# Hybrid HGRN2 and differential-attention block on one core: the order of the first loads, and half of two modulation parts as direct matmuls

## The reference

```python
mod = silu(c) @ w_ada + b_ada
shift, scale, gate = split(mod, 3)
h = rms_norm(x, g_pre) * (1.0 + scale) + shift
proj = h @ w_in          # 6144 columns: hq hf hi hg dq dk dv dg ma mb
# branch A: HGRN2, chunked recurrence, per-head RMSNorm, * silu(hg)
# branch B: differential causal attention, per-head RMSNorm, * silu(dg)
y = sigmoid(ma) * (o_a @ w_branch_a) + sigmoid(mb) * (o_b @ w_branch_b)
x = x + gate * rms_norm(y @ w_out, g_post)
```

## Time and profile before

| | |
|---|---|
| time, median of 3 runs | 908.14 us (908.01 to 912.44) |
| profiled execution: time | 908.02 us |
| profiled execution: span of the trace | 906.2 us |
| mean granted TensorE clock | 0.989 |
| TensorE matmul busy | 853.7 us, 94% |
| VectorE busy | 575.3 us, 63% |
| ScalarE busy | 441.5 us, 49% |
| GpSimd busy | 447.8 us, 49% |

### The profile page before, as it was taken

The page is one execution under the profiler, slowest core; times in us unless marked ns, Lnnn a source line. Parts: engine busy times, 40 slices in busy tenths (PEclk is TensorE's granted clock), DMA queues, the critical chain, the costliest instruction groups (busy, mean ns, idle before and its releaser), DMA issues. The chain is left out here.

```text
span 906.2 us, 12968 instructions
## 1 busy us (share of the span) xinstructions
PE 853.7 (94%) x4829; PEld 671.6 (74%) x4829; DVE 575.3 (63%) x691; ACT 441.5 (49%) x808; POOL 447.8 (49%) x348
## 2 busy tenths in 40 slices
PE   2899899999999999999999999999999999999996
PEld 2678677777777777777777777777788788778885
DVE  3888984788684897866886948746200622982222
ACT  7676322885445865437864446754445700321111
POOL 6054665455555445654454555556788564730000
PEclk9899899999999999999999999999999999999999
DMA  9914221102110120121021021201321731111231
GB/s 329 327 48 140 70 70 47 48 1 71 47 48 24 47 70 1 48 70 46 3 71 47 2 69 47 69 10 39 101 62 46 279 140 47 35 59 47 102 108 70
DMA packets 74481, 68.10 MB, mean 75 GB/s; under 512 B 3700, under 2 KB 65204, under 8 KB 74420
## 3 DMA queue, kind: packets, MB, share of 16 engines
q1 hardware_dynamic: 74304, 67.25, 23.0%
q10 hardware_dynamic: 116, 0.03, 0.0%
HBM read 58.88 MB, written 8.39 MB: 74 GB/s over the span
## 5 line engine op out<-in xcount | busy, mean ns | idle before, releaser
L595 POOL TENSOR_TENSOR w_lo<-w_raw,w_hi 128x512 fp32r<-128x512 f32 x140 | 193.0, 1380 | 261.4 <-ACT w_hi L1144 259.9
L879 PE MATMUL pj<-b_hi,w_hi 128*128 128x512 f32 x616 | 263.0, 427 | 2.7 <-DVE dk L1467 1.5
L881 PE MATMUL pj<-b_hi,w_lo 128*128 128x512 f32 x616 | 242.2, 393 | 0.0
L880 PE MATMUL pj<-b_lo,w_hi 128*128 128x512 f32 x616 | 241.8, 392 | 0.0
L879 PEld LDWEIGHTS pj<-b_hi,w_hi 128*128 128x128 f32 x616 | 116.4, 189 | 40.1 <-issue 10.2
L881 PEld LDWEIGHTS pj<-b_hi,w_lo 128*128 128x128 f32 x616 | 116.2, 189 | 26.2
L880 PEld LDWEIGHTS pj<-b_lo,w_hi 128*128 128x128 f32 x616 | 116.8, 190 | 22.7 <-issue 3.8
L1144 ACT ACTIVATE w_hi<-w_raw 128x512 fp32r<-128x512 f32 x132 | 82.8, 628 | 64.0 <-PE pj L881 57.6
L576 POOL TENSOR_TENSOR w_raw<-w_raw,w_raw 128x512 f32<-128x512 f32 x66 | 91.8, 1391 | 2.9
L1159 ACT ACTIVATE p<-sp,cols 128x1024 f32<-128x1024 f32 (+7 forms) x64 | 46.8, 737 | 0.8
L1301 ACT ACTIVATE y_hi<-y 128x1024 fp32r<-128x1024 f32 x8 | 8.5, 1062 | 74.8 <-DVE y L1668 74.8
(11 more groups left out here) (250 smaller groups left out, 1709.9 us busy)
## 6 DMA issues: line engine op xcount, KB each, us to landing
w_raw<-in_w_in SPq DMA_DIRECT2D x96, 256.0 KB, 4.1
x_in<-in_x SPq DMA_DIRECT2D x8, 512.0 KB, 7.1
ada<-in_w_ada SPq DMA_DIRECT2D x16, 256.0 KB, 7.0
ada<-in_w_ada SPq DMA_DIRECT2D x8, 512.0 KB, 8.0
ada_g<-in_w_ada SPq DMA_DIRECT2D x8, 512.0 KB, 3.8
wo_raw<-in_w_out SPq DMA_DIRECT2D x8, 512.0 KB, 4.0
res<-in_x SPq DMA_DIRECT2D x8, 512.0 KB, 4.2
out_x<-y2n SPq DMA_DIRECT2D x8, 512.0 KB, 2.9
```

The lines of the kernel that those rows point to most:

```text
L595: pool.tensor_tensor(w_lo[slot(v)][:, :], raw[:, :], w_hi[slot(v)][:, :].bitcast(F32), ALU.subtract).then_inc(s_wlo, 1)
L879: pe.matmul(bank[:, :], wh, part(b_hi[m], kk), start=(fresh and kk == 0), stop=False, skip_group_check=True)
L880: pe.matmul(bank[:, :], wh, part(b_lo[m], kk), start=False, stop=False, skip_group_check=True)
L881: last = pe.matmul(bank[:, :], wl, part(b_hi[m], kk), start=False, stop=(kk == 3), skip_group_check=True)
```

## The change

The loads are issued in another order: four tiles of x, weights of group 0, piece 0 of w_ada, weights of group 1, piece 1, then the second half of x, then (behind a wait for s_modp, the first columns of the modulation) piece 2 and the rest. In pieces 0 and 1 half of the row tiles (4 to 7, and 0 to 3) are no longer summed by VectorE; TensorE multiplies them itself with one column of silu(c), as sixteen matmuls of one column per piece, and sums in PSUM. Piece 1 gets another PSUM bank. Transposes of the first half run tile by tile as the tiles are scaled; two warming matmuls come earlier. The second half of x is squared, scaled, transposed and used later, with products of j = 0 and 1 between its transposes; the products of kh = 1 for j = 0 and 1 have kk outside. ScalarE takes the fourth tile's scaling and starts with a Sqrt.

```diff
+DIRECT = [[4, 5, 6, 7], [0, 1, 2, 3]]
+ADDS = [4, 8, 16]
...
-        XT_BANKS = [0, 1, 2, 3, 4, 5, 6, 0, 4, 5, 6, 4, 5, 6, 4, 5]
+        mod_banks = [mod_bank, first_banks[0][1], mod_bank]
+        XT_BANKS = [0, 1, 2, 3, 4, 5, 6, 0, 6, 4, 5, 6, 6, 6, 6, 6]
...
+            load_x(0)
+            load_half(0, 0)
+            load_piece(0)
+            load_half(1, 0)
+            load_piece(1)
+            load_x(1)
+            sp_.wait_ge(s_modp, 1)
+            load_piece(2)
...
+            def mod_direct(p, kk):
+                a, b = PIECES[p]
+                pe.wait_ge(s_ada[p][kk // 2], 32)
+                for z in range(2):
+                    for e in range(a, b):
+                        c0 = z * P * (b - a) + P * (e - a)
+                        last = pe.matmul(mod_banks[p][:, KT * z + e:KT * z + e + 1], ada[p][kk][:, c0:c0 + P], c_silu[:, kk:kk + 1],
+                                         start=(kk == DIRECT[p][0] and z == 0 and e == a), stop=False, skip_group_check=True)
...
-            for n in range(KT):
-                x_block(n)
-            pe.wait_ge(s_const, N_CONST)
-            pe.wait_ge(s_vec, 1)
-            mod_columns(0)
-            pe.wait_ge(s_xt, KT)
             for _ in range(2):
                 pe.matmul(first_banks[3][0], ident[:, :], sc[:, 0:HALF], start=True, stop=True)
+            for t in range(4):
+                if t == 3:
+                    pe.wait_ge(s_xnb, 1)
+                else:
+                    pe.wait_ge(s_xna, t + 1)
+                for n in range(KT - 1):
+                    last = pe.transpose(xt_bank[n][:, t * P:(t + 1) * P], x_in[:, t * D + n * P:t * D + (n + 1) * P], ident[:, :])
+                    if t == 3:
+                        last.then_inc(s_xtr, 1)
+                if t == 1:
+                    pe.wait_ge(s_gain, 1)
+                if t >= 1:
+                    mod_direct(0, DIRECT[0][t - 1])
+            mod_direct(0, DIRECT[0][3])
+            mod_columns(0)
+            x_block(KT - 1)
+            pe.wait_ge(s_const, N_CONST)
+            pe.wait_ge(s_xt, 5)
+            for kk in DIRECT[1]:
+                mod_direct(1, kk)
+            pe.wait_ge(s_xt, KT)
...
-                elif kk < 3:
-                    for n in range(4):
-                        x_block(KT + 4 * (kk - 1) + n)
-            mod_columns(2)
+            for n in range(4):
+                x_block(KT + n)
+            pe.wait_ge(s_xt, KT + 3)
+            for kk in range(4):
+                pe.wait_ge(s_bl, 4 + kk + 1)
+                for j in range(2):
+                    last = first_product(j, 0, 1, kk)
+                    if kk == 3:
+                        last.then_inc(s_proj, 1)
+                x_block(KT + 4 + kk)
+                if kk == 1:
+                    mod_columns(2)
             pe.wait_ge(s_xt, 2 * KT)
-            for j in range(4):
+            for j in range(2, 4):
...
-            for j, th in ((0, 0), (1, 0), (0, 1), (1, 1)):
-                pe.wait_ge(s_wlo, 5 + j)
+            for th in range(2):
                 for kk in range(4):
-                    if j == 0:
-                        pe.wait_ge(s_bl, 8 + 4 * th + kk + 1)
-                    last = first_product(j, 1, th, kk)
-                last.then_inc(s_proj if th else s_first, 1)
+                    pe.wait_ge(s_bl, 8 + 4 * th + kk + 1)
+                    for j in range(2):
+                        if kk == 0 and th == 0:
+                            pe.wait_ge(s_wlo, 5 + j)
+                        last = first_product(j, 1, th, kk)
+                        if kk == 3:
+                            last.then_inc(s_proj if th else s_first, 1)
...
+            act.activation(t_o, ones[:, 0:1], ACT.Sqrt)
+            for t in range(4):
+                square(t)
+            root(0)
...
+            scale_x(3)
+            act.activation(t_o, ones[:, 0:1], ACT.Sqrt)
+            for n in range(KT):
+                x_out(n)
+            act.wait_ge(s_mod, 1)
+            blocks(0, 1)
+            blocks(1, 2)
+            square(4)
+            square(5)
+            act.wait_ge(s_mod, 2)
+            blocks(2, 4)
+            for t in range(6, NT):
                 square(t)
             root(1)
             act.wait_ge(s_rsq, 2)
+            scale_x(7)
+            x_out(KT)
+            blocks(4, 5)
+            for n in range(KT + 1, KT + 3):
                 x_out(n)
+            blocks(5, 6)
+            x_out(KT + 3)
+            x_out(KT + 4)
+            blocks(6, 7)
+            x_out(KT + 5)
+            blocks(7, 8)
+            x_out(KT + 6)
+            x_out(KT + 7)
             act.wait_ge(s_mod, 3)
             blocks(8, 16)
...
             norm(0)
             dve.wait_ge(s_rsq, 1)
+            scale_x(0)
+            scale_x(1)
+            dve.wait_ge(s_sigc, 1)
+            then(dve.tensor_tensor(c_silu, c_col, c_sig, ALU.mult))
...
+            scale_x(2)
+            for kk in range(4):
                 add_ada(0, kk)
             mod_piece(0)
+            add_ada(1, 4)
             block_low(0)
             add_ada(1, 5)
             block_low(1)
             add_ada(1, 6)
             add_ada(1, 7)
+            mod_piece(1)
+            block_low(2)
+            block_low(3)
             add_ada(2, 0)
             add_ada(2, 1)
+            norm(1)
+            dve.wait_ge(s_rsq, 2)
+            for t in range(4, 7):
+                scale_x(t)
+            for kk in range(2, 4):
+                add_ada(2, kk)
+            block_low(4)
             add_ada(2, 4)
             add_ada(2, 5)
+            block_low(5)
             add_ada(2, 6)
             add_ada(2, 7)
+            block_low(6)
+            block_low(7)
             mod_piece(2)
```

More of the change, by code:

```diff
@@ L477, in _, with load_x, load_piece @@
             w_mod = w_ada[0, :, 0:2 * D].rearrange("k (z f) -> k z f", z=2)
-            for half in range(2):
+            def load_x(half):
                 for t in range(4 * half, 4 * half + 4):
                     sp_.dma_start(x_in[:, t * D:(t + 1) * D], x_v[t * P:(t + 1) * P, :]).then_inc(s_xl[t], 16)
-                load_half(half, 0)
-            for p, (a, b) in enumerate(PIECES):
+            def load_piece(p):
+                a, b = PIECES[p]
                 for kk in range(KT):
-                    if p == 2 and kk == 0:
-                        sp_.wait_ge(s_acc, KT)
                     sp_.dma_start(ada[p][kk][:, :].rearrange("p (z f) -> p z f", z=2),
                                   w_mod[kk * P:(kk + 1) * P, :, a * P:b * P]).then_inc(s_ada[p % 2][kk // 2], 16)
+            load_x(0)
[6 more added lines that the diff above has]
+            load_piece(2)
             for half in range(2):
@@ L799, in mod_columns @@
                         c0 = 2 * P * a + z * P * (b - a) + P * (e - a)
-                        last = pe.matmul(mod_bank[:, KT * z + e:KT * z + e + 1], acc[:, c0:c0 + P], ones[:, 0:1],
-                                         start=True, stop=True)
+                        last = pe.matmul(mod_banks[p][:, KT * z + e:KT * z + e + 1], acc[:, c0:c0 + P], ones[:, 0:1],
+                                         start=(p == 2), stop=True, skip_group_check=True)
                 last.then_inc(s_modp, 1)
@@ L999, in blocks @@
                 block_high(e1 - 1)
-            square(0)
-            square(1)
+            act.wait_ge(s_const, 3)
+            act.activation(t_o, ones[:, 0:1], ACT.Sqrt)
+            for t in range(4):
+                square(t)
+            root(0)
             act.wait_ge(s_vec, 1)
@@ L1007, in _ @@
             act.activation(one_less_lb, lb_diff, ACT.Sigmoid, scale=-1.0).then_inc(s_sigc, 1)
-            square(2)
-            square(3)
-            root(0)
-            for t in range(4, NT):
+            act.wait_ge(s_rsq, 1)
+            scale_x(3)
[10 more added lines that the diff above has]
+            for t in range(6, NT):
                 square(t)
@@ L1014, in _ @@
             act.wait_ge(s_rsq, 2)
-            for n in range(4):
+            scale_x(7)
+            x_out(KT)
+            blocks(4, 5)
+            for n in range(KT + 1, KT + 3):
                 x_out(n)
-            scale_x(4)
-            x_out(4)
-            x_out(5)
-            scale_x(5)
-            x_out(6)
-            x_out(7)
-            act.wait_ge(s_mod, 1)
-            blocks(0, 2)
-            scale_x(6)
-            scale_x(7)
-            act.wait_ge(s_mod, 2)
-            blocks(2, 4)
-            for n in range(KT, KT + 4):
-                x_out(n)
-            blocks(4, 5)
-            for n in range(KT + 4, 2 * KT):
-                x_out(n)
-            blocks(5, 8)
+            blocks(5, 6)
[6 more added lines that the diff above has]
+            x_out(KT + 7)
             act.wait_ge(s_mod, 3)
@@ L1376, in _ @@
             dve.wait_ge(s_rsq, 1)
-            for t in range(4):
-                scale_x(t)
-            norm(1)
-            for kk in range(KT):
+            scale_x(0)
```

(13 more changed lines are left out.)

43 lines of the change are left out of this document (17 added, 26 removed).

## The result

The changed kernel takes 914.40 us (median of 9 runs, 912.91 to 917.44) against 908.44 for the kernel before (9 runs, 906.75 to 912.44). The ratio is 1.0059, 95% interval 1.0041 to 1.0078 (ratios here are formed from all the runs; that of the two medians would be 1.0066). The profiled execution took 913.71 us at a span of 911.8; the one of before 908.02 at 906.2. So the forecast of 906.4 and its range up to 911.5 are missed on the slow side.

The account below looks back on a forecast made before the run. DVE's unbroken run from M6's low part (76.03) to PE's wait ending at 97.88 was taken to bound the kernel. Starting it at 74.4 gained 1.6 us: span 906.2 to 904.6, plus 1.8 outside, 906.4 us; range 902.6 to 911.5.

Parts of the forecast that it names:

- Direct columns: TensorE's one-column matmuls for the modulation: 0.12 us each assumed, range up to 0.22, from a row of 16 lasting 1.95.
- Start: Loads to first product: first columns near 18, first product at 22.2 against 31.08, 8.9 us earlier.
- Loads: Loading phase: first half of x at 8.0 us, part 0 by 15, part 1 by 22, second half of x by 28.
- Middle: From mod_columns(1) at 26.8 to ACT's blocks 8 to 15 at 53.1, 2.9 us later than before.
- The spell at the low clock: In the middle, after mod_columns(2)'s sixteen columns: one slow-clock spell adding 1.6 us before blocks 8 to 15.
- Blocks 8 to M6: From blocks 8 at 53.1 to DVE's M6 low part at 74.4: 21.3 us, the kh = 1 order delaying the q copy.
- From there to the end: From M6's low part to the end: DVE never waits until 97.88, so 1.6 us gained there reaches the end.
- forecast lead of 1.6 us: At DVE's M6 low part: start at 74.4 instead of 76.03, taken whole off the span.
- Slow middle: Rival, PE from 38 to 58 us: low clock between bursts of two products, +3.1 us, 911.1 us; chance 0.13.
- The low spell moves: Rival: clock falls near 85 ahead of L740, spell after 97.88 goes, 1.6 + 3.3 us gained, 903.1; chance 0.08.
- The lead passes whole: Rival: hidden DVE slack between 76 and 98, so PE's own 3.7 us gain counts, 902.6 us; chance 0.10.
- Nothing arrives: Rival: loads 2 us later than estimated, or a second short low-clock spell, 908.2 us; chance 0.15.

Follow-up runs that it names:

- second experiment: The changed kernel with no direct columns at all, VectorE summing parts 0 and 1 wholly: 916.05 us, ratio 1.0063.
- the one execution with a trace: The kernel before with ScalarE making M6's high part before forget(0, 1) instead of after it: 909.28 us, ratio 0.9990.
- the warmed version: The changed kernel with part 1 summed by VectorE and two 512-column warming matmuls ahead of the first product: 911.35 us, ratio 1.0017.

## Why the prediction was wrong, step by step

The step that failed is the start, up to mod_columns(1), which stood in the sum at 26.8 and came at 32.8. In it the direct columns were mis-sized: sixteen were priced at 1.9 us and took 3.4 in part 0, and those of part 1, which have no term of their own in the sum, took 6 us, of which 2.0 to 3.8 us arrived. The place that passes a loss on, M6's low part, was named rightly.

The parts of the change, each by what M6's low part does when it alone is added to the version above it:

| version | M6's low part at, us | step | time, us | ratio |
|---|---|---|---|---|
| kernel before | 76.03 | | | 1 |
| new loads alone | 81.35 | +5.3 | 914.82 | 1.0052 |
| and direct columns of part 0 | 79.31 | -2.0 | 911.59 | 1.0031 |
| and the new middle | 78.11 | -1.2 | 910.70 | 1.0017 |
| and direct columns of part 1 (the changed kernel) | 80.08 (again: 81.50) | +2.0 (+3.4) | 914.40 | 1.0059 |

The steps sum to 4.05 and are of single executions. Three executions with the same start have their first product at 26.55, 27.61 and 29.16, so a step of 1 or 2 us is no more than a sign; the ratios of the runs have the same order, and give +4.7, -1.9, -1.3 and +3.8 us for the four steps. The direct columns of part 0 are worth 4.0 with the new middle (second experiment) and 2.0 with the old one (3.0 where blocks 8 start); why a third of it is lost between there and M6 in the old order stays open. The step "new middle" includes the new order of the kh = 1 products.

**Direct columns, the term that was mis-sized.** I took sixteen for 1.9 us, since a row "x16" lasted 1.95. An f32 matmul is two records, so sixteen are 32 records: 3.4 us at the full clock (part 0: 0.88, 0.81 and 1.71 us) and 5.3 to 6.8 us where the clock falls (part 1). The count could have been had from the rows of before: four columns of `mod_columns(0)` in the code stand as x8. For the columns of part 1 the sum has no term: its 22.2 for the first product goes through ACT and DVE, as if they lay wholly in PE's wait for the first low part. That wait covers 3 of the 6 us: the low part started at 23.84 and took 0.69, the first product came at 27.61. So 3 us remained in this execution, 3.4 against the version with an equally early fall of the clock, 3.8 by the ratios.

**Start.** First columns at 20.3 to 21.2 in place of 18: the direct columns of part 0 cost 1.5 us more by the same count, PE waited 0.91 us for part 0's loads, and DVE's product for silu(c) took 1.23 us and so held the third tile. Without part 1's columns the first product starts at 25.6, so at most 3.4 of the 5.4 us by which it came late are here, and 2.0 or more are part 1's columns. The chain from the end of part 0's columns over affine, high and low part takes 4.1 us there (21.5 to 25.6), near the 4.2 that I had. The low clock over the first twelve matmuls of the products was nowhere in the sum: mod_columns(1) came 5.2 us behind the first product, and I had 4.6.

**Loads.** DVE's first sum of part 1 waited for its load until 23.00, where the same rate as in the sum (part 1 in by 22) gives 20.6; the first tile of the second half of x was there at 27.11, where it gives 23.4. So they were 2.4 and 3.7 us late. In the changed kernel this was hidden: ACT, which had waited 1.94 us for x, waited 4.63 more for part 1's columns afterwards, and these were released by PE.

**Middle.** From mod_columns(1) to blocks 8 I had 26.3 us, measured 25.2. The four waits of PE that I had as 1.9, 0.65, 0.55 and 0.8 are 1.82, 0.36, 0.43 and 0.69 (a fifth is 0.19). The spell at the low clock (1.6 us) did not come. But I had only compared the end with the old one, 53.1 with 50.25, and read the 2.9 us as a detail of PE's and ACT's order. The run with the new loads alone shows 5.2 us at this point. That they come from the work on the later half of x is read from DVE's and ACT's rows there; no run moved that half by itself (the run also has the transposes row group by row group and ACT's new start). The direct columns of part 0 pay back a part of it.

**Blocks 8 to M6.** 21.3 forecast, 22.1 measured. The order of kh = 1 was charged with 2 us and saves 1.8; that the sum was nearly right here is luck. Forecast 74.4, measured 80.08: +6.0 at mod_columns(1), -1.1 in the middle, +0.8 here.

**From there to the end.** That M6's low part passes delays on holds in the rows: +2.36 becomes +2.3 in the span, +4.05 stays 4.07 up to 442 us, and ten of thirteen traces take 362.0 to 362.6 us from there to the copy of q. For leads, on which the forecast rested, it stays open: -3.04 became -0.7 in the one execution with a trace, but by a low clock that the kernel before shows without a lead. What the forecast lead of 1.6 us would have been worth can't be said from these runs.

**Rivals.** *Slow middle* fell for the changed kernel, whose clock stays 1.00 from 38 to 58. The waits between its bursts were 0.19 to 1.82 us. The page of the Trainium skill that the forecast cited ("TensorE: Matmul & The Clock Gate", section "HAM oscillation — how this bites in real kernels") tells of waits of about 3 to 5 us, so the middle here is no test of it; I had stretched it to shorter ones. In the warmed version one wait of 1.82 was followed by 0.73 over 6 us. At the start the clock fell between 20.3 and 22.7, where PE had had no wait since 15.5 at the latest, in or behind rows of one-column matmuls. So it did in the kernel before: the forecast named half a microsecond of idle time ahead of the sixteen columns' row at 47.87, but PE idled 0.11 us in the 4.9 us ahead of it, and the clock fell at 50.0. *The low spell moves* came half true: PE no longer waits 3 us at L753, but waits 2.7 us further on, and the clock is 0.83 from 106 to 116. The waits of PE in the kernel after, 80 to 114 us (us in total, times, longest; they answer rows 4):

```profile
PE pj L929 <- DVE stage L1523: 2.7, 1, 2.7
PE by L753 <- DVE sc L1584: 2.3, 2, 1.5
```

*The lead passes whole* was not put to the test, since nothing arrived early. *Nothing arrives* named the loads and would have given 908.2; what it lacked was a reason that the middle could lose more than the start wins.

No version tried is faster than the kernel before. The best of the changed ones, without direct columns of part 1, is level with it within its interval.

## What to carry to other kernels

Count a row's instructions against the code before pricing with it: a record need not be an instruction. Loading first what is first needed moves the work on the later half too, here out of a time in which PE had to wait anyway (7.71 us up to 16.03 in the kernel before) and into the one in which DVE had none to give; cost the preparation of the deferred half at its new place, on every engine. And measure what a lead at the deciding instruction is worth before building a forecast on it: here delays passed it whole, while a lead of 3.04 us brought 0.7 us in its trace and between 0 and 2.6 us by its runs. One trace of each kernel would have misled: two executions of the kernel before lay 4.1 us apart.

## What the runs showed of the hardware

- A matmul of one column with f32 operands lasts 0.21 us at the full clock and 0.42 at the low one, as two records and counted from start to start. With PE busy 6.00 of 6.00 us the clock went to 1.2 GHz (0.50) within the row of sixteen in three executions (after, the one with the old kh = 1 order, the one with the columns done twice); in the second execution of the changed kernel it had done so 2 us ahead of the row, and in the version without that row as well (20.5).
- A wait of PE of 2.0 us near 725 was followed by 1.00 over 720 to 740 in four traces and by 0.91 in nine, the same code among both.
- DVE's product of two 128x512 operands takes 0.69 us alone (103.79) and 1.75 to 1.78 beside GpSimd's splits and weight sums (94.58 and 111.42, all in the kernel before). The Trainium skill, page "SBUF — State Buffer", section "SBUF: two separate sides", says that the two engines take turns at a shared port. DVE's c·sigmoid(c) on 8 columns, 0.17 us in the kernel before (L1327), took 1.23 us at 13.25 in the changed kernel, beside a split of GpSimd that started at 12.86.
